# The one-hot product of an expert choice goes to GpSimd, with two one-hot tiles in place of one

## The chip, the cores and the metric

One core of one Trainium2 chip runs the whole program. The time is the device time of one execution in microseconds (us). Engines are called by the profile's names: PE (TensorE; PEld is its weight load), DVE (VectorE), ACT (ScalarE), POOL (GpSimd), SP (SyncE, which here only issues transfers).

## What is computed

Three transformer layers run one after the other on 256 tokens of width 1024, all in f32. The first two layers end in a mixture of 16384 tiny experts, and the change lies there:

```python
q  = (h @ wq).reshape(B, S, PEER_HEADS, 2, half)          # 8 heads, two halves
s1 = einsum('bshd,hnd->bshn', q[..., 0, :], keys[:, 0])   # 128 scores a half
v1, i1 = top_k(s1, 16);  v2, i2 = top_k(s2, 16)
cand = v1[..., :, None] + v2[..., None, :]                # sums of pairs
sc, j = top_k(cand, 16)
e1 = take_along_axis(i1, j // 16); e2 = take_along_axis(i2, j % 16)
experts = e1 * 128 + e2;  gates = softmax(sc)
act = gelu(einsum('td,ted->te', ht, u[experts]))
out = einsum('te,ted->td', gates * act, v[experts])
```

## The kernel before

The kernel is written engine by engine, each engine's instructions in an order fixed by the program, with semaphores between the engines. Nothing is scheduled by a planner.

**The expert layer.** It gathers nothing. It computes `gelu` of h times every row of the table u: 128 blocks of 128 experts, block `j` into column `j` of the array `av`. After that it multiplies `av` by a sparse matrix of gates and multiplies the result by the table v, again in 128 blocks. The profile calls nearly everything in SBUF `mem`, since the tiles are slices of one tensor.

**A u-block.** A table piece of 128x1024 comes by a transfer into a ring. ACT (`hi`) rounds it to `r_sh`, DVE (`lo`) forms the rest `r_sl`. PE's `block_T` multiplies by both: 16 matmuls with `r_sh`, then, after a wait for "lo", 8 with `r_sl`. `r_sh` and `r_sl` have two buffers each, so ACT begins `hi(n)` when PE is done with block n-2. After each block ACT takes its result through `gelu`.

**The choice of experts.** Which experts a token wants is found during these same blocks, on DVE. `choices` is a Python generator: for each of two tiles of 128 tokens it takes 16 top-16 selections of 128 scores (`side`), forms the 50 candidate sums of each head (`cand`) with the numbers of their experts (`ecand`), takes each head's top 16 of 50, and then turns 16 places into 16 expert numbers. For this last step, of each head h: a one-hot tile of 16 x 50 is made by comparing places with `iota` (EQ), multiplied by `ecand` (MUL), and summed over the 50 (`tensor_reduce` into `EF`). All are 128x800 in the trace, and all three used one tile, `hot`.

**What sets the order on DVE.** `peer_ve` walks over `j` = 0 to 127. At each `j`, called a slot below, it issues `lo` of the next block and then as many steps of `choices` as this rule asks for. Each step gives its cost by `yield`; `COST` is their sum, so that the steps end just before `j` = 75:

```python
for j in range(128):
    lo(ve, (U + V)[j + 1])
    while spent * (C_FROM - 3) < COST * (j + 1):     # C_FROM = 78
        did = next(pick, None)
        ...
        spent += did
```

**After the choice.** "e12" (expert numbers split in two) and "gates" (softmax) are awaited by PE's transposes ahead of blocks 76 and 77 ("eTp"); ACT copies these to `eT` at `j` = 77 and 78. Only then does POOL have work in this layer: `peer_po` makes a part of the one-hot tiles `oneA` for the gate matrix. Until then it only helps with the norm ahead of the layer. `J_EARLY` and `J_LATE` say from which block on ACT's `gelu` would write over the tiles of the choice, and what it waits for there.

Of the kernel before, what the change touches and what calls it, by code (L numbers as in the profile page):

```python
# [19 lines left out]
NP = len(PAIRS)  # L20
# [206 lines left out]
MUL, ADD, SUB, MAX, MIN, EQ = ALU.mult, ALU.add, ALU.subtract, ALU.max, ALU.min, ALU.is_equal  # L227
# [58 lines left out]
def build(nc, io, ctx):  # L286
# [28 lines left out]
    def C(name, rows=128):  # L315
        lo, hi = CST[name]
        return cst[0:rows, lo:hi]

    def P(name, i=None):
        lo, hi = COL[name]  # L320
        return col[:, lo:hi] if i is None else col[:, lo + i:lo + i + 1]
# [163 lines left out]
    def norm_po(po, k, gain, shift=None):  # L485
        po.wait_ge("rr", k)
        for c in (3, 7):
            h = hT[:, c, :]
            po.wait_ge(*po.tensor_tensor(h, xT[:, c, :], rr_, MUL).then_inc("scaledP"))
            if shift is None:  # L490
                po.tensor_scalar(h, h, gain(c), MUL).then_inc("hP", k, c)
            else:
                po.tensor_scalar(h, h, gain(c), MUL, shift(c), ADD).then_inc("hP", k, c)
        for c in (3, 7):
            po.wait_ge("hhi", k, c)
            po.tensor_tensor(hlov[:, c, :], hT[:, c, :], hhiv[:, c, :].bitcast(F32), SUB).then_inc("hloP", k, c)
# [32 lines left out]
    o = 0  # L529

    def take(n):
        nonlocal o
        o += n
        return arena[:, o - n:o]
# [354 lines left out]

    av = mem[:, 0:32768].rearrange("p (j t) -> p j t", j=128)  # L890
    A0 = 32768 - A
    o = A0 - (4096 + 6 * 256 + 8 * (3 * 32 + 2 * (NP + 2)) + 700 + 16 * NP) - 4096
    keysb = take(2048)
    keys = keysb.rearrange("p (h n) -> p h n", h=16)
    qTb = [chunks(take(1024), 4) for _ in range(2)]
# [2 lines left out]
    SC, EF, GT, E1, E2 = (take(256) for _ in range(5))  # L898
    EI = take(256).bitcast(U32)
    s2 = [take(128) for _ in range(2)]  # L900
    cand, ecand = (take(8 * (NP + 2)).rearrange("p (h c) -> p h c", h=8) for _ in range(2))
    cand2 = take(NP + 2)[:, 0:NP]
    hot = take(16 * NP)
    v16 = take(256).rearrange("p (h k) -> p h k", h=8)
    i16 = take(256).bitcast(U32).rearrange("p (h k) -> p h k", h=8)
    f16 = take(256).rearrange("p (h k) -> p h k", h=8)
    p16 = take(128).bitcast(U32)
    p16f = take(128)
    st = take(32)
    assert o <= A0, o  # L910
    o = A0
# [8 lines left out]
    iota = C("iota")  # L920
# [8 lines left out]
    def peer(layer):  # L929
        k = 1 + 2 * layer  # L930
# [9 lines left out]
        def raw_tile(src):  # L940
            tiles.append([src, ("raw_free", layer, len(tiles) - 4) if len(tiles) >= 4 else was[0]])
            return len(tiles) - 1
# [9 lines left out]
        for j in range(128):  # L952
            if j < 127:
                V.append(table("v", j + 1))
            if layer == 0 and 4 <= j < 124 and (j - 4) % 2 == 0 and (j - 4) % 10 < 8:
                pc, q = (j - 4) // 10, (j - 4) % 10 // 2
                at, w = flat(WEIGHTS["ada"])[pc]
                i = raw_tile(io["ada"][at:at + 128 * w].rearrange("(p f) -> p f", p=128)[:, 1024 * q:1024 * q + 1024])
# [30 lines left out]
        def peer_po(po):  # L989
            norm_po(po, k, lambda c: P(f"f{layer}", c))  # L990
            po.wait_ge("x_out", layer)
            for g in range(64):
                s = 4 * (g % 2)
                po.wait_ge("eT", layer, g // 32)
                if g >= 2:
                    po.wait_ge("prod", layer, g - 2)
                for i in range(2):
                    n = 4 * g + i
                    d = po.tensor_scalar(oneA[:, s + i, :], iota, eT[0][:, n:n + 1], EQ, eT[2][:, n:n + 1], MUL)
                d.then_inc("hotP", layer, g)  # L1000
# [92 lines left out]
        def side(ve, t, h, i):  # L1093

            s, k0 = scores[:, t, 2 * h + i, :], 16 * i
            va, vb = v16[:, h, k0:k0 + 8], v16[:, h, k0 + 8:k0 + 16]
            ia, ib = i16[:, h, k0:k0 + 8], i16[:, h, k0 + 8:k0 + 16]
            ve.wait_ge("scores", layer, h // 2, t)
            ve.wait_ge(*ve.max(va, s).then_inc("dveC"))
            d = ve.match_replace(s2[i], va, s, -3e38).then_inc("dveC")  # L1100
            ve.max_index(ia, va, s)
            ve.wait_ge(*d)
            ve.wait_ge(*ve.max(vb, s2[i]).then_inc("dveC"))
            return ve.max_index(ib, vb, s2[i]).then_inc("dveC")

        def choices(ve):

            g, s = GT.rearrange("p (h k) -> p h k", h=16), SC.rearrange("p (h k) -> p h k", h=16)
            for t in range(2):
                for h in range(8):  # L1110
                    for i in range(2):
                        d = side(ve, t, h, i)
                        yield 15
                ve.wait_ge(*d)
                ve.wait_ge(*ve.tensor_copy(f16, i16).then_inc("dveC"))
                ve.wait_ge(*ve.tensor_scalar(f16[:, :, 0:16], f16[:, :, 0:16], 128.0, MUL).then_inc("dveC"))
                yield 6
                for dst, src in ((cand, v16), (ecand, f16)):
                    off = 0
                    for i0, i1, n in ((0, 1, 16), (1, 2, 8), (2, 3, 5), (3, 4, 4), (4, 5, 3), (5, 8, 2), (8, 16, 1)):  # L1120
                        m = i1 - i0
                        dv = dst[:, :, off:off + m * n].rearrange("p h (i j) -> p h i j", i=m)
                        x = src[:, :, i0:i1].rearrange("p h (i o) -> p h i o", o=1).broadcast_to([128, 8, m, n])
                        z = src[:, :, 16:16 + n].rearrange("p h (o j) -> p h o j", o=1).broadcast_to([128, 8, m, n])
                        d = ve.tensor_tensor(dv, x, z, ADD)
                        off += m * n
                    d = d.then_inc("dveC")
                    yield 14
                ve.wait_ge(*d)
                for h in range(8):  # L1130
                    c, sc16, p = cand[:, h, 0:NP], SC[:, 128 * t + 16 * h:128 * t + 16 * h + 16], p16[:, 16 * h:16 * h + 16]
                    ve.wait_ge(*ve.max(sc16[:, 0:8], c).then_inc("dveC"))
                    d = ve.match_replace(cand2, sc16[:, 0:8], c, -3e38).then_inc("dveC")
                    ve.max_index(p[:, 0:8], sc16[:, 0:8], c)
                    ve.wait_ge(*d)
                    ve.wait_ge(*ve.max(sc16[:, 8:16], cand2).then_inc("dveC"))
                    d = ve.max_index(p[:, 8:16], sc16[:, 8:16], cand2).then_inc("dveC")
                    yield 13
                ve.wait_ge(*d)
                d = ve.tensor_copy(p16f, p16).then_inc("dveC")  # L1140
                if t:
                    ve.tensor_tensor(g, s, s[:, :, 0:1].broadcast_to([128, 16, 16]), SUB).then_inc("gmax", layer)
                hv = hot.rearrange("p (k c) -> p k c", k=16)
                for h in range(8):
                    ve.wait_ge(*d)
                    i = ve.tensor_tensor(hv, p16f[:, 16 * h:16 * h + 16].rearrange("p (k o) -> p k o", o=1).broadcast_to([128, 16, NP]),
                                         iota[:, 0:NP].rearrange("p (o c) -> p o c", o=1).broadcast_to([128, 16, NP]), EQ).then_inc("dveC")
                    yield 10
                    ve.wait_ge(*i)
                    i = ve.tensor_tensor(hv, hv, ecand[:, h, 0:NP].rearrange("p (o c) -> p o c", o=1).broadcast_to([128, 16, NP]),  # L1150
                                         MUL).then_inc("dveC")
                    yield 10
                    ve.wait_ge(*i)
                    d = ve.tensor_reduce(EF[:, 128 * t + 16 * h:128 * t + 16 * h + 16], hv, ADD).then_inc("dveC")
                    yield 10
            ve.wait_ge(*d)
            ve.wait_ge(*ve.tensor_copy(EI, EF).then_inc("dveC"))
            ve.tensor_scalar(E2.bitcast(U32), EI, 127, ALU.bitwise_and)
            ve.wait_ge(*ve.tensor_scalar(E1.bitcast(U32), EI, 7, ALU.logical_shift_right).then_inc("dveC"))
            ve.tensor_copy(E2, E2.bitcast(U32))  # L1160
            ve.tensor_copy(E1, E1.bitcast(U32)).then_inc("e12", layer)
            yield 15
            ve.wait_ge("gexp", layer)
            ve.wait_ge(*ve.tensor_reduce(st[:, 0:16], g, ADD).then_inc("dveC"))
            ve.wait_ge(*ve.reciprocal(st[:, 16:32], st[:, 0:16]).then_inc("dveC"))
            ve.tensor_tensor(g, g, st[:, 16:32].rearrange("p (h o) -> p h o", o=1).broadcast_to([128, 16, 16]), MUL).then_inc("gates", layer)
            yield 10

        COST = 2 * (16 * 15 + 6 + 28 + 8 * 13 + 8 * 30) + 25

        def peer_ve(ve):
            norm_ve(ve, k, WQ[0][0], lambda c: P(f"f{layer}", c))
# [23 lines left out]
            for j in range(128):  # L1196
                lo(ve, (U + V)[j + 1])
                while spent * (C_FROM - 3) < COST * (j + 1):
                    did = next(pick, None)
# [1102 lines left out]
```

## Time and profile before

| | |
|---|---|
| median of 3 runs | 2711.04 us (2706.79 to 2711.13) |
| the profiled execution | 2704.2 us, of which its span is 2702.4 us |
| PE busy | 2496.0 us, 92% of the span |
| DVE busy | 1720.0 us, 64% |
| ACT busy | 1297.0 us, 48% |
| POOL busy | 466.0 us, 17% |
| u-blocks 2 to 75 or so, first expert layer | about 290 to 520 us of the span |
| the same, second expert layer | about 1374 to 1604 us |

A share is a mean over stages with different limits. What the change is worth has to be read inside the two stretches in the last lines of the table. Matmuls overlap in the records (0.28 us each, started every 0.12 us), so a busy PE says that it had work, and its pace is seen in the distance between starts.

### The profile page before, as it was taken

What the parts mean: (1) busy time and instruction counts of PE and PEld (TensorE: products, weight loads), DVE (VectorE), ACT (ScalarE), POOL (GpSimd) and SP (SyncE); (2) the same over time, 40 slices, a digit from 0 to 9 for tenths busy, and PEclk for the clock granted to TensorE, in tenths of its full rate; (3) what the DMA queues carried; (4) which work ended last, traced back from release to release, by engine and by line L of the source; (5) the groups of instructions that cost most, each with busy time, mean ns of one, the idle gap of its engine ahead of it and who ended that gap; (6) DMA issues with size and microseconds to landing.
All of it is one profiled execution on the core that took longest, in us unless ns stands there. A gap on an engine that the chain in (4) does not pass through costs nothing.

```text
span 2702.4 us, 47390 instructions
## 1 busy us (share of the span) xinstructions
PE 2496.0 (92%) x19556; PEld 2407.8 (89%) x19556; DVE 1720.0 (64%) x3162; ACT 1297.0 (48%) x2447; POOL 466.0 (17%) x390
## 2 busy tenths in 40 slices
PE   7277999999999999888899999999999988997899
PEld 6267999999999999865799999999999977787899
DVE  3864699877777767534469987775555543534654
ACT  4124544576544444444444456654444443453543
POOL 4900000188500000000000018850000000001000
PEclk9668999999999999999899999999999988999999
DMA  6103355544477777530235554446556553223352
GB/s 239 50 32 125 102 182 185 164 133 129 138 265 250 252 240 251 225 125 32 94 125 183 185 172 131 128 141 196 185 182 185 182 212 134 85 94 122 128 187 79
DMA packets 93220, 422.17 MB, mean 156 GB/s; under 512 B 10296, under 2 KB 12880, under 8 KB 85072
## 3 DMA queue, kind: packets, MB, share of 16 engines
q1 hardware_dynamic: 93008, 419.16, 46.8%
q8 instruction: 156, 2.56, 0.4%
q14 instruction: 56, 0.46, 0.0%
HBM read 415.96 MB, written 3.16 MB: 155 GB/s over the span
## 4 chain that ended last, share of the span: by engine, by line
PE 88%; DVE 6%; ACT 4%; issue 1%; POOL 0%; DMA 0%; SPq 0%; DVEq 0%; POOLq 0%; ACTq 0%
PE PS L170 88%; ACT mem L181 2%; DVE mem L192 2%; ACT r_sh L181 1%; DVE mem L184 1%; DVE r_sl L184 1%; DVE hT L192 1%; PE PS L173 0%; DVE mem L204 0%; ACT L180 0%; DVE xT L184 0%; DVE mem L198 0%; ACT r_hhi L181 0%; POOL hT L184 0%; DVE hT L188 0%
## 5 line engine op out<-in xcount | busy, mean ns | idle before, releaser
L184 DVE TENSOR_TENSOR r_sl<-mem,r_sh 128x1024 fp32r<-128x1024 f32 (+3 forms) x742 | 891.8, 1203 | 756.0 <-ACT r_sh L181 753.1
L181 ACT ACTIVATE r_sh<-mem 128x1024 fp32r<-128x1024 f32 (+3 forms) x742 | 765.1, 1033 | 510.7 <-PE PS L170 469.4
L170 PE MATMUL PS<-r_hhi,r_sh 128*128 128x256 f32 x3280 | 840.3, 292 | 101.1 <-ACT r_sh L181 66.4
L170 PE MATMUL PS<-r_hlo,r_sh 128*128 128x256 f32 (+1 forms) x3152 | 790.7, 287 | 17.6 <-DVE r_hlo L184 15.8
L170 PEld LDWEIGHTS PS<-r_hhi,r_sh 128*128 128x128 f32 x3280 | 644.2, 196 | 110.2 <-issue 57.2
L170 PEld LDWEIGHTS PS<-r_hlo,r_sh 128*128 128x128 f32 (+1 forms) x3152 | 616.5, 196 | 20.2 <-DVE r_hlo L184 17.6
L170 PE MATMUL PS<-r_ch,r_sh 128*128 128x256 f32 x2048 | 504.1, 283 | 0.0
L170 PE MATMUL PS<-r_cl,r_sh 128*128 128x256 f32 x2048 | 503.2, 283 | 0.7 <-DVE r_cl L184 0.7
L170 PE MATMUL PS<-r_hhi,r_sl 128*128 128x256 f32 x3280 | 469.9, 286 | 2.0 <-DVE r_sl L184 2.0
L181 ACT ACTIVATE mem<-PS 128x256 f32<-128x256 f32 (+22 forms) x629 | 215.2, 351 | 512.1 <-PE PS L170 485.9
L189 POOL TENSOR_SCALAR xT<-cst,mem 128x128 f32<-128x128 f32 x256 | 327.5, 1291 | 621.9 <-ACT mem L181 558.1
L170 PEld LDWEIGHTS PS<-r_hhi,r_sl 128*128 128x128 f32 x3280 | 431.8, 195 | 2.8 <-DVE r_sl L184 2.5
L170 PEld LDWEIGHTS PS<-r_cl,r_sh 128*128 128x128 f32 x2048 | 393.1, 192 | 1.1 <-DVE r_cl L184 1.1
L170 PEld LDWEIGHTS PS<-r_ch,r_sh 128*128 128x128 f32 x2048 | 393.0, 192 | 0.0
L170 PE MATMUL PS<-r_ch,r_sl 128*128 128x256 f32 x2048 | 289.7, 283 | 0.0
L170 PEld LDWEIGHTS PS<-r_ch,r_sl 128*128 128x128 f32 x2048 | 265.2, 192 | 0.0
L170 PE MATMUL PS<-mem 64*128 64x128 f32 (+8 forms) x824 | 134.5, 319 | 3.2 <-DVE mem L204 1.1
L184 POOL TENSOR_TENSOR hT<-xT,small 128x256 f32<-128x256 f32 x12 | 9.9, 822 | 736.1 <-ACT small L181 736.1
L170 PE MATMUL PS<-xT 128*128 128x128 f32 x1024 | 130.8, 276 | 4.0 <-DVE xT L184 4.0
L170 PEld LDWEIGHTS PS<-mem 64*128 64x128 f32 (+4 forms) x824 | 100.9, 172 | 33.6 <-issue 17.8
L170 PEld LDWEIGHTS PS<-xT 128*128 128x128 f32 x1024 | 123.4, 193 | 4.3 <-issue 4.3
L181 ACT ACTIVATE mem<-mem 128x128 f32<-128x128 f32 (+9 forms) x117 | 62.5, 544 | 134.6 <-DVE mem L198 75.7
(126 smaller groups left out, 2238.2 us busy)
## 6 DMA issues: line engine op xcount, KB each, us to landing
mem<-in_u SPq DMA_DIRECT2D x256, 512.0 KB, 3.6
mem<-in_v SPq DMA_DIRECT2D x256, 512.0 KB, 4.3
mem<-in_w SPq DMA_DIRECT2D x16, 2048.0 KB, 8.2
mem<-in_ada SPq DMA_DIRECT2D x48, 512.0 KB, 4.1
mem<-in_in SPq DMA_DIRECT2D x9, 2048.0 KB, 8.4
mem<-in_wq SPq DMA_DIRECT2D x8, 2048.0 KB, 8.5
mem<-in_od_in SPq DMA_DIRECT2D x6, 2048.0 KB, 9.2
mem<-in_ev_in SPq DMA_DIRECT2D x5, 2048.0 KB, 10.6
```

The source lines that it names most:

```text
L170: return self.did(self.e and self.e.matmul(out, lhsT, rhs, start=start, stop=stop, skip_group_check=skip))
L181: return self.did(self.e and self.e.activation(out, in_, func, **kw))
L184: return self.did(self.e and self.e.tensor_tensor(out, a, b, op))
L189: return self.did(self.e and self.e.tensor_scalar(out, a, s1, s2, op0, op1))
L192: return self.did(self.e and self.e.scalar_tensor_tensor(out=out, in0=a, scalar=s, in1=b, op0=op0, op1=op1))
```

## The change

DVE still makes the one-hot tile of a head (EQ) and still sums it (`tensor_reduce`). The product with `ecand` is now a POOL instruction, 8 a tile, 16 a layer, 32 in all, written ahead of POOL's other work of the layer. There are two one-hot tiles, used in turn. On DVE the sum of head h-1 now stands behind the EQ of head h. EQ announces "asked", POOL's product "found", the sum "chosen"; EQ of head h waits for "chosen" of head h-2, which is two sums back in the tile and the DVE instruction just ahead of it. `COST` is smaller by the steps that left, so all steps of the choice are spread over the same 75 slots at 1101/75 = 14.7 units a slot, where it was 1261/75 = 16.8.

The second tile takes 800 more columns, so all tiles of the choice begin 800 columns lower; with that `J_EARLY` goes from 77 to 74 and `J_LATE` from 93 to 90.

```diff
-    o = A0 - (4096 + 6 * 256 + 8 * (3 * 32 + 2 * (NP + 2)) + 700 + 16 * NP) - 4096
+    o = A0 - (4096 + 6 * 256 + 8 * (3 * 32 + 2 * (NP + 2)) + 700 + 32 * NP) - 4096
...
-    hot = take(16 * NP)
+    hot = [take(16 * NP).rearrange("p (k c) -> p k c", k=16) for _ in range(2)]
...
             po.wait_ge("x_out", layer)
+
+            for t in range(2):
+                for h in range(8):
+                    po.wait_ge("asked", layer, t, h)
+                    po.tensor_tensor(hot[h % 2], hot[h % 2], ecand[:, h, 0:NP].rearrange("p (o c) -> p o c", o=1).broadcast_to([128, 16, NP]),
+                                     MUL).then_inc("found", layer, t, h)
...
-                d = ve.tensor_copy(p16f, p16).then_inc("dveC")
+                ve.tensor_copy(p16f, p16).then_inc("places", layer, t)
...
-                hv = hot.rearrange("p (k c) -> p k c", k=16)
-                for h in range(8):
-                    ve.wait_ge(*d)
-                    i = ve.tensor_tensor(hv, p16f[...], iota[...], EQ).then_inc("dveC")
-                    yield 10
-                    ve.wait_ge(*i)
-                    i = ve.tensor_tensor(hv, hv, ecand[...], MUL).then_inc("dveC")
-                    yield 10
-                    ve.wait_ge(*i)
-                    d = ve.tensor_reduce(EF[:, 128 * t + 16 * h:128 * t + 16 * h + 16], hv, ADD).then_inc("dveC")
-                    yield 10
-            ve.wait_ge(*d)
+                for h in range(9):
+                    if h < 8:
+                        if t or h >= 2:
+                            ve.wait_ge("chosen", layer, (8 * t + h - 2) // 8, (h - 2) % 8)
+                        ve.wait_ge("places", layer, t)
+                        ve.tensor_tensor(hot[h % 2], p16f[...], iota[...], EQ).then_inc("asked", layer, t, h)
+                        yield 10
+                    if h:
+                        ve.wait_ge("found", layer, t, h - 1)
+                        d = ve.tensor_reduce(EF[:, 128 * t + 16 * h - 16:128 * t + 16 * h], hot[(h - 1) % 2], ADD).then_inc("chosen", layer, t, h - 1)
+                        yield 10
+            ve.wait_ge("chosen", layer, 1, 7)
...
-        COST = 2 * (16 * 15 + 6 + 28 + 8 * 13 + 8 * 30) + 25
+        COST = 2 * (16 * 15 + 6 + 28 + 8 * 13 + 8 * 20) + 25
```

How the instructions then stand on DVE, at the start of the second tile's one-hot steps in the first expert layer. `r_sl` is `lo` of a block and opens a slot; `mem<-mem,cst 128x800` is EQ, `mem<-mem 128x800` the product, `TENSOR_REDUCE` the sum. Before:

```order
L195 CAST mem<-mem 128x128
L184 TENSOR_TENSOR mem<-mem 128x256
L184 TENSOR_TENSOR mem<-mem,cst 128x800
L184 TENSOR_TENSOR mem<-mem 128x800
L184 TENSOR_TENSOR r_sl_53<-mem,r_sh_51 128x1024
L198 TENSOR_REDUCE mem<-mem 128x16
L184 TENSOR_TENSOR r_sl_54<-mem,r_sh_52 128x1024
L184 TENSOR_TENSOR mem<-mem,cst 128x800
L184 TENSOR_TENSOR mem<-mem 128x800
```

And with the change, the same place and the cycle of four slots that follows:

```order
L184 TENSOR_TENSOR mem<-mem,cst 128x800
L184 TENSOR_TENSOR r_sl_54<-mem,r_sh_52 128x1024
L184 TENSOR_TENSOR mem<-mem,cst 128x800
L198 TENSOR_REDUCE mem<-mem 128x16
L184 TENSOR_TENSOR r_sl_53<-mem,r_sh_51 128x1024
L184 TENSOR_TENSOR mem<-mem,cst 128x800
L184 TENSOR_TENSOR r_sl_54<-mem,r_sh_52 128x1024
L198 TENSOR_REDUCE mem<-mem 128x16
L184 TENSOR_TENSOR mem<-mem,cst 128x800
L184 TENSOR_TENSOR r_sl_53<-mem,r_sh_51 128x1024
L198 TENSOR_REDUCE mem<-mem 128x16
L184 TENSOR_TENSOR r_sl_54<-mem,r_sh_52 128x1024
```

The products are gone from between EQ and sum, and a head's sum comes two steps and at least one `lo` after its EQ. A slot holds one or two steps, in the pattern [EQ, sum], [EQ], [sum, EQ], [sum].

On POOL, in each of the two expert layers, between the norm and the one-hot tiles of the gate matrix:

```order
 L188 TENSOR_SCALAR hT<-hT,col 128x256
 L184 TENSOR_TENSOR r_hlo<-hT,r_hhi 128x256 x2
+L184 TENSOR_TENSOR mem<-mem 128x800 x16
 L189 TENSOR_SCALAR xT<-cst,mem 128x128 x128
```

Sixteen products came in where POOL had nothing; the instructions around them stand as they did.

## Rows read from the trace of the kernel before

**Rows 1.** Busy time in the two stretches of u-blocks with the choice.
```profile
core 0: us, PE busy (x) PEld busy (x) DVE busy (x) ACT busy (x) POOL busy (x), PEclk, DMA share, GB/s
290.00:510.00 220.00, 219.87 (x1834) 219.66 (x1834) 195.05 (x540) 106.26 (x158) 0.00 (x0) 1.00 0.55 173
1374.00:1594.00 220.00, 219.87 (x1834) 219.66 (x1833) 195.06 (x540) 106.29 (x158) 0.00 (x0) 1.00 0.56 173
475.00:505.00 30.00, 30.00 (x252) 30.00 (x252) 29.03 (x29) 15.53 (x23) 0.00 (x0) 1.00 0.57 180
```

**Rows 2.** All waits from 290 to 505 us: us in total, times, longest.
```profile
ACT mem L181 <- PE PS L170: 113.3, 74, 2.5
DVE r_sl L184 <- ACT r_sh L181: 20.3, 33, 6.5
```

**Rows 3.** PE in order of time: low halves (`r_sl`) of two successive blocks.
```profile
start us, us, engine line op out<-in xcount [idle before <-releaser]
442.66 1.12 PE L170 MATMUL PS<-r_hhi,r_sl 128*128 128x256 f32 x8
...
445.54 1.12 PE L170 MATMUL PS<-r_hhi,r_sl 128*128 128x256 f32 x8
```

**Rows 4.** ACT in order of time: one gelu and the `hi` behind it.
```profile
440.94 0.38 ACT L181 ACTIVATE mem<-PS 128x256 f32<-128x256 f32 x1 [1.55 <-PE PS L170]
441.22 1.05 ACT L181 ACTIVATE r_sh<-mem 128x1024 fp32r<-128x1024 f32 x1
```

**Rows 5.** DVE in order of time: a `lo` with slack, then a stretch of one-hot steps.
```profile
442.30 1.23 DVE L184 TENSOR_TENSOR r_sl<-mem,r_sh 128x1024 fp32r<-128x1024 f32 x1 [0.20 <-ACT r_sh L181]
...
479.94 1.22 DVE L184 TENSOR_TENSOR r_sl<-mem,r_sh 128x1024 fp32r<-128x1024 f32 x1
481.07 0.98 DVE L198 TENSOR_REDUCE mem<-mem 128x16 f32<-128x800 f32 x1
482.08 0.99 DVE L184 TENSOR_TENSOR mem<-mem,cst 128x800 f32<-128x800 f32 x1
482.99 1.22 DVE L184 TENSOR_TENSOR r_sl<-mem,r_sh 128x1024 fp32r<-128x1024 f32 x1
484.13 0.98 DVE L184 TENSOR_TENSOR mem<-mem 128x800 f32<-128x800 f32 x1
```

**Rows 6.** POOL in order of time, in the convolution of the first layer.
```profile
54.61 1.90 POOL L184 TENSOR_TENSOR mem<-mem,col 128x512 f32<-128x512 f32 x1
56.59 1.29 POOL L184 TENSOR_TENSOR mem<-mem 128x512 f32<-128x512 f32 x1
57.97 1.90 POOL L184 TENSOR_TENSOR mem<-mem,col 128x512 f32<-128x512 f32 x1
...
61.32 1.04 POOL L184 TENSOR_TENSOR mem<-mem,col 128x512 f32<-128x512 f32 x1
```

**Rows 7.** DVE in order of time, the same stretch.
```profile
54.18 1.43 DVE L184 TENSOR_TENSOR r_sl<-mem,r_sh 128x1024 fp32r<-128x1024 f32 x1 [1.93 <-ACT r_sh L181]
57.06 1.91 DVE L184 TENSOR_TENSOR r_sl<-mem,r_sh 128x1024 fp32r<-128x1024 f32 x1 [1.45 <-ACT r_sh L181]
```

**Rows 8.** POOL in order of time, third layer: a start behind DVE, a 256-column operation.
```profile
2441.02 0.74 POOL L184 TENSOR_TENSOR hT<-mem 128x256 f32<-128x256 f32 x1 [240.97 <-DVE mem L184]
2442.28 0.73 POOL L184 TENSOR_TENSOR r_hlo<-hT,r_hhi 128x256 fp32r<-128x256 f32 x1 [0.53 <-ACT r_hhi L181]
```

**Rows 9.** DVE in order of time: the operation that released the first of these.
```profile
2440.45 0.43 DVE L184 TENSOR_TENSOR mem<-PS,mem 128x256 f32<-128x256 f32 x1 [0.69 <-PE PS L170]
```

**Rows 10.** DVE and PE in order of time: "gates" written, and the transposes of block 76.
```profile
517.54 0.42 DVE L184 TENSOR_TENSOR mem<-mem 128x256 f32<-128x256 f32 x1
...
518.86 0.49 PE L173 MATMUL PS<-cst,mem 128*128 128x128 f32 x3
...
530.29 2.71 PE L170 MATMUL PS<-xT 128*128 128x128 f32 x16 [1.99 <-DVE xT L184]
```

**Rows 11.** PE in order of time, third layer: one of seven such waits in a row.
```profile
2446.96 0.36 PE L170 MATMUL PS<-r_qa,r_sh 128*128 128x256 f32 x1 [1.05 <-ACT r_sh L181]
```

**Rows 12.** Busy time and granted clock around a short and a long PE wait.
```profile
2446.00:2450.00 4.00, 3.04 (x24) 2.88 (x24) 2.16 (x4) 1.35 (x4) 1.47 (x2) 1.00 0.02 4
528.00:534.00 6.00, 4.01 (x25) 3.84 (x24) 5.69 (x10) 4.04 (x14) 2.47 (x3) 0.79 0.45 122
```

More of the change, by code:

```diff
@@ L1139, in choices @@
                 ve.wait_ge(*d)
-                d = ve.tensor_copy(p16f, p16).then_inc("dveC")
+                ve.tensor_copy(p16f, p16).then_inc("places", layer, t)
                 if t:
                     ve.tensor_tensor(g, s, s[:, :, 0:1].broadcast_to([128, 16, 16]), SUB).then_inc("gmax", layer)
-                hv = hot.rearrange("p (k c) -> p k c", k=16)
-                for h in range(8):
-                    ve.wait_ge(*d)
-                    i = ve.tensor_tensor(hv, p16f[:, 16 * h:16 * h + 16].rearrange("p (k o) -> p k o", o=1).broadcast_to([128, 16, NP]),
-                                         iota[:, 0:NP].rearrange("p (o c) -> p o c", o=1).broadcast_to([128, 16, NP]), EQ).then_inc("dveC")
-                    yield 10
-                    ve.wait_ge(*i)
-                    i = ve.tensor_tensor(hv, hv, ecand[:, h, 0:NP].rearrange("p (o c) -> p o c", o=1).broadcast_to([128, 16, NP]),
-                                         MUL).then_inc("dveC")
-                    yield 10
-                    ve.wait_ge(*i)
-                    d = ve.tensor_reduce(EF[:, 128 * t + 16 * h:128 * t + 16 * h + 16], hv, ADD).then_inc("dveC")
-                    yield 10
-            ve.wait_ge(*d)
+                for h in range(9):
[3 more added lines that the diff above has]
+                        ve.wait_ge("places", layer, t)
+                        ve.tensor_tensor(hot[h % 2], p16f[:, 16 * h:16 * h + 16].rearrange("p (k o) -> p k o", o=1).broadcast_to([128, 16, NP]),
+                                         iota[:, 0:NP].rearrange("p (o c) -> p o c", o=1).broadcast_to([128, 16, NP]), EQ).then_inc("asked", layer, t, h)
+                        yield 10
[4 more added lines that the diff above has]
+            ve.wait_ge("chosen", layer, 1, 7)
             ve.wait_ge(*ve.tensor_copy(EI, EF).then_inc("dveC"))
```

## The prediction

> **What bounds the kernel now.** I read the busy time of the two stretches of u-blocks first. PE is busy for 219.87 of 220 us in both, at the full clock; DVE for 195, POOL for nothing [rows 1]. The list of waits of 290 to 505 us has ACT waiting for PE and DVE for ACT, and no row at all in which PE waits [rows 2]. PE's low halves come 445.54 - 442.66 = 2.88 us apart [rows 3], which is 24 matmuls of 0.12 us. So a slot lasts 2.88 us, PE sets it, and the 31.6 us that the 32 products cost DVE (0.98 us each) are under PE's work. To take them away can give nothing here. What the change can do is make DVE late, so the next thing to read is how late DVE may be.
>
> A block that ends at about 440.74 (442.66 less 16 matmuls) lets ACT do its gelu and then `hi`, at 441.22 for 1.05 us [rows 4]. `lo` follows at 442.30 and is through at 443.53 [rows 5]. PE wants it for the low half at 445.54 [rows 3]. DVE's lead is 2.0 us, and it cannot be more, since `hi` waits for PE. It is the reserve of all that follows.
>
> **DVE without its product.** From start to start DVE spends 1.13 us on a `lo`, 1.01 on a sum ahead of an EQ that waits for it, 0.91 on an EQ ahead of something that doesn't wait for it, 1.14 on another `lo` [rows 5]. The new order repeats in four slots with three heads: [lo, EQ, sum], [lo, EQ], [lo, sum, EQ], [lo, sum]. That is 4 x 1.14 + 3 x 0.91 + 2 x 0.91 + 1.01 = 10.1 us, against 4 x 2.88 = 11.5 us. Alone it fits, with 1.4 us to spare in a cycle (before, 29.03 of 30 us were busy at the one-hot steps [rows 1]). The added wait of a sum for "found" would be hidden too: two steps and a `lo`, some 3 us, lie between a head's EQ and its sum. Queued behind that wait is `lo`, for which PE waits.
>
> **What the product takes on POOL.** No row shows 128x800. A two-tensor operation of 256 columns takes 0.73 us [rows 8] and of 512 columns 1.29 us, while it was ahead of DVE's `lo` [rows 6]: 2.19 ns a column, so 1.29 + 288 x 2.19 ns = 1.92 us. Below lies the form with an operand that is one value per row, 1.04 us for 512 [rows 6]; with the same fixed 0.17 us that gives 0.17 + 800 x 1.70 ns = 1.53 us. Above lies the 0.73 us scaled whole, 800/256 x 0.73 = 2.28 us, as if nothing of it were fixed. I take 1.92: both operands of the new product vary along the columns, as in the 1.29 us row. The GPSIMD Engine Reference of the Trainium skill (section 3.1) gives 2.6 cycles an element for two inputs; at its 1.2 GHz that is an estimate of 1.73 us for 800, by which the sum below would be about 5 us and not 11. The trace's 2.19 ns a column is the same slope; the difference is the fixed part.
>
> **What it takes from DVE.** The rows of the convolution show the two engines excluding each other. `lo` began at 57.06, took 1.91 us in place of 1.23 and ended at 58.97: it really ran from 57.74, which is 0.14 us before POOL's 56.59 + 1.29 = 57.88 [rows 6, 7]. POOL's next operation took 1.90 us in place of 1.04: it ran from 58.83, again 0.14 us before the end of `lo`. The one at 54.61 did the same behind the `lo` that ended at 55.61. So each waits for the other's whole operation, less 0.14 us. `lo` and EQ read two SBUF tensors, like the operations of these rows. The sum reads one; no row has one beside POOL. I take it as free of this. If it isn't, that is the dear rival below. The SBUF page of the Trainium skill (Who interferes with whom) says that a DVE instruction with at most one SBUF input outside the 2-port modes doesn't contend, and a reduction never; no run so far shows it.
>
> POOL starts 0.14 us after DVE's end (2440.45 + 0.43 to 2441.02 [rows 8, 9]). Three places in a cycle then cost DVE a wait, counted from the start of an EQ:
> - [EQ, sum], then `lo`: the product runs from 0.98 + 0.14 = 1.12 and lets go at 1.12 + 1.92 - 0.14 = 2.90. `lo` could start at 1.82. Wait 1.08.
> - [EQ], then `lo`: `lo` is on at 0.91, ahead of POOL. The product runs from 0.91 + 1.23 - 0.14 = 2.00 and lets go at 3.78. The sum starts at 2.05, and the EQ behind it could at 3.06. Wait 0.72.
> - [sum, EQ], `lo`, [sum], `lo`: the same, but the last `lo` could start at 2.96. Wait 0.82.
>
> Together 2.6 us. A cycle is 10.1 + 2.6 = 12.7 us against 11.5: DVE falls back 1.2 us every three heads.
>
> **The walk through the slots.** I carried this on slot by slot: DVE starts `lo` when it and `hi` are ready, PE starts a low half when `lo` is through, and the lead never passes 2.0 us. First tile: the first `lo` behind a lone EQ finds DVE idle and POOL already in and waits 1.4 us; the lead falls from 2.0 to 0.6 us within four slots. Then PE waits 0.60, 0.07, 1.15 and 0.26 us, in sum 2.1. Second tile: the copy of the places and the extra subtraction put the first EQ later, the first `lo` waits the whole 1.8 us, the lead is 0.25, and PE waits 0.94, 0.07, 1.15, 0.07 and 1.10 us, in sum 3.3. (Each 1.1 to 1.2 is one cycle's deficit.) A layer loses 5.3 us, the two 10.7 us.
>
> Does the clock add to it? PE waits of 1.05 us in the third layer, seven in a row, 4.1 us apart, leave the granted clock at 1.00, its upper level [rows 11, 12]. After 2.0 us of waiting at 528.3 it was lower, 0.79 on average over 6 us [rows 10, 12]. The waits forecast here stay below 1.2 us, so I add nothing.
>
> **What costs nothing.** "gates" is written by 517.96, 0.9 us ahead of the transposes of block 76 [rows 10]. In the new order these steps stand in the same slots, 73 and 74, and have only to come before a PE that is itself later; in the walk they are 1.3 us ahead. The "gmax" for ACT's exponential moves from slot 59 to 62 and is wanted at 70. The lower `J_EARLY` and `J_LATE` wait for the last scores and for `eT`, both over by then. POOL's next work is wanted only after "eT". PE, ACT and SP keep their order, and no transfer is added.
>
> **The sum.** 2704.2 us of the profiled execution (span 2702.4 and 1.8 around it) + 10.7 = 2714.9. The median shown lies 6.8 us higher, so I say 2711.04 + 10.7, about 2721.5 us. Each 0.1 us of product above 1.7 is worth 32 x 0.1 = 3.2 us; below 1.6 the lead swallows nearly all: 1.53 gives +0.6, 2.28 gives +22.
>
> **Rivals.**
> - **Hidden after all**, 2711 to 2714. The product is near 1.53 us, or the exclusion costs less than in the convolution, because here POOL's operations come singly. For it: POOL would be busy for about half the time at most, and the break-even product is 1.6 us. Against: the four fits to 0.14 us. Chance 0.28.
> - **A longer product**, some 2.3 us, or PE waits long enough to lower the clock: 2711 + 22 = 2733. Sixteen runs of 50 columns are a shape no row has. Against: nothing in the rows charges for the number of runs. Chance 0.11.
> - **The sum is blocked as well.** Then nothing of the product is under DVE work: another 0.7 us a head by the same walk, +34 us in all, 2745. No row speaks to it. Chance 0.08.
> - **Faster.** PE's one long wait here is the 1.99 us at 530.29 for the first one-hot tiles, with the low clock behind it [rows 10, 12]: some 3.3 us a layer. If an earlier end of the choice removed it, 2704.5. But the new `COST` spreads the steps over the same 75 slots, and the transposes at 518.86 didn't wait; it would need "gates" a slot earlier and the transposes moved. Chance 0.03.
>
> **How the numbers follow.** The likeliest case, PE losing 4 to 17 us because DVE waits for POOL, has 0.5, with 2715 to 2728 as its own range. 0.2% of this time, about what a measurement can tell, is 5.4 us, so the low end of that case counts as no change: I put 0.02 of its chance there. Slower is then 0.48 + 0.11 + 0.08 = 0.67, the same 0.30, faster 0.03. For 8 in 10 the range leaves out the blocked sum and the faster case and half of the tail: 2709 to 2734.
>
> **What would show it.** In the new profile: POOL products of about 1.9 us, longer where a `lo` is ahead; `lo` and EQ in the one-hot slots with some 2 us in place of 1.2 and 1.0, the sums still 0.98; some nine PE waits for `r_sl` a layer, in two clusters near 375 to 410 and 485 to 520 us of the span, 5 us in sum; the rest of the span shifted and otherwise the same. The prediction is wrong if `lo` beside a product keeps its 1.23 us, if the product is off 1.9 us by more than 0.2, or if the sums lengthen.

## The result and the profile after

The changed kernel took 2718.5 us in the median of 20 runs, the kernel before 2708.0 us in the same comparison: a ratio of 1.0033 (95% interval 1.0025 to 1.0041), 8.9 us slower (6.8 to 11.1). Two of the 20 runs of the changed kernel were slow, 3129.5 and 3535.2 us at a granted clock of 0.734 and 0.645 where the other 18 had 0.952 to 0.958; the ratio leaves them out, and the 8.9 us is the ratio times 2708.0, not the distance of the medians (10.5). Its profiled execution took 2713.9 us with a span of 2711.9, 9.5 us more than the span before.

The busy time in the two stretches of u-blocks, which answers to [rows 1]:

```profile
core 0: us, PE busy (x) PEld busy (x) DVE busy (x) ACT busy (x) POOL busy (x), PEclk, DMA share, GB/s
290.00:510.00 220.00, 218.95 (x1821) 218.28 (x1820) 190.13 (x522) 104.74 (x157) 33.62 (x15) 1.00 0.56 171
1380.00:1600.00 220.00, 218.82 (x1818) 217.98 (x1818) 191.92 (x525) 105.17 (x157) 35.83 (x16) 1.00 0.58 174
```

PE has 13 to 16 matmuls fewer in the same 220 us (x1821 and x1818, 1834 before), some 0.12 us each. DVE is only 3 to 5 us less busy, though 15 or 16 products of 0.98 us left it: part of its busy time is now waiting, which the profile counts as busy. The clock is at its upper level throughout, so none of this loss is the clock's.

POOL in order of time, three successive products of the first tile:

```profile
389.65 1.76 POOL L184 TENSOR_TENSOR mem<-mem 128x800 f32<-128x800 f32 x1 [2.07 <-DVE mem L184]
393.48 2.68 POOL L184 TENSOR_TENSOR mem<-mem 128x800 f32<-128x800 f32 x1 [2.07 <-DVE mem L184]
397.09 2.67 POOL L184 TENSOR_TENSOR mem<-mem 128x800 f32<-128x800 f32 x1 [0.93 <-DVE mem L184]
```

The product takes 1.76 us when nothing is ahead of it (14 of the 32), and 2.67 when a `lo` is (18 of the 32). DVE beside these, a cycle of four slots, which answers to [rows 5]:

```profile
389.49 0.97 DVE L198 TENSOR_REDUCE mem<-mem 128x16 f32<-128x800 f32 x1
390.38 2.11 DVE L184 TENSOR_TENSOR r_sl<-mem,r_sh 128x1024 fp32r<-128x1024 f32 x1
392.42 0.98 DVE L184 TENSOR_TENSOR mem<-mem,cst 128x800 f32<-128x800 f32 x1
393.32 1.22 DVE L184 TENSOR_TENSOR r_sl<-mem,r_sh 128x1024 fp32r<-128x1024 f32 x1
394.45 0.97 DVE L198 TENSOR_REDUCE mem<-mem 128x16 f32<-128x800 f32 x1
395.46 1.55 DVE L184 TENSOR_TENSOR mem<-mem,cst 128x800 f32<-128x800 f32 x1
396.93 1.21 DVE L184 TENSOR_TENSOR r_sl<-mem,r_sh 128x1024 fp32r<-128x1024 f32 x1
398.07 0.97 DVE L198 TENSOR_REDUCE mem<-mem 128x16 f32<-128x800 f32 x1
398.96 1.88 DVE L184 TENSOR_TENSOR r_sl<-mem,r_sh 128x1024 fp32r<-128x1024 f32 x1
400.77 0.98 DVE L184 TENSOR_TENSOR mem<-mem,cst 128x800 f32<-128x800 f32 x1
401.67 0.97 DVE L198 TENSOR_REDUCE mem<-mem 128x16 f32<-128x800 f32 x1
402.56 2.10 DVE L184 TENSOR_TENSOR r_sl<-mem,r_sh 128x1024 fp32r<-128x1024 f32 x1
```

Read the second column. The `lo` at 390.38 lasts 2.11 us in place of 1.22: the product ran from 389.65 to 391.41. The EQ at 395.46 lasts 1.55 in place of 0.98, under the product that ended at 396.16. The `lo` at 398.96 lasts 1.88. The sums stay at 0.97, also the one at 389.49, with a product beside it for most of its time. And PE's low halves:

```profile
401.28 1.12 PE L170 MATMUL PS<-r_hhi,r_sl 128*128 128x256 f32 x8
404.72 1.22 PE L170 MATMUL PS<-r_hhi,r_sl 128*128 128x256 f32 x8 [0.40 <-DVE r_sl L184]
407.70 1.12 PE L170 MATMUL PS<-r_hhi,r_sl 128*128 128x256 f32 x8
```

The `lo` at 402.56 was through at 404.66, the low half began at 404.72, 3.44 us after the one before and not 2.88. The same reading of all low halves from 310 to 520 us and from 1395 to 1605 us gives the distances that are over 2.88 us. In us, by which they are over:

| | first tile | second tile | sum |
|---|---|---|---|
| forecast, each layer | 0.60, 0.07, 1.15, 0.26 | 0.94, 0.07, 1.15, 0.07, 1.10 | 5.3 |
| first expert layer | 0.07, 0.56, 0.10, 0.06 | 0.42, 0.09, 0.55, 0.09, 0.22, 0.10 | 2.3 |
| second expert layer | 0.07, 0.56, 0.09, 0.06 | 0.41, 0.10, 0.56, 0.09, 0.22, 0.09 | 2.2 |

(One of 0.35 us a layer, at ACT's exponential, is there before and after and left out.) So the choice costs 4.5 us. Of the 9.5 us by which this span grew, 5 us lie elsewhere, and what they are is taken up behind the experiments on the choice.

### The profile page after: what moved, and what is told of

It reads as the page before. It is cut to its first block, busy times and chain, and to the rows that moved or that the text cites. A ratio compares the mean times of both kernels' runs of the same rounds, so it can differ in the third digit from the quotient of the medians.

```text
span 2711.9 us, 47394 instructions
## 1 busy us (share of the span) xinstructions
PE 2500.0 (92%) x19556; PEld 2408.6 (89%) x19556; DVE 1713.0 (63%) x3130; ACT 1296.5 (48%) x2447; POOL 544.3 (20%) x422
## 4 chain that ended last, share of the span: by engine, by line
PE 83%; DVE 10%; ACT 5%; issue 1%; POOL 1%; DMA 0%; SPq 0%; DVEq 0%; POOLq 0%; ACTq 0%
PE PS L170 83%; DVE r_sl L184 3%; DVE mem L184 2%; ACT mem L181 2%; DVE mem L192 2%; ACT r_sh L181 2%; DVE mem L198 1%; DVE hT L192 0%; ACT L180 0%; POOL r_hlo L184 0%; PE PS L173 0%; DVE mem L204 0%; ACT r_hhi L181 0%; DVE xT L184 0%; POOL hT L184 0%
## 5 line engine op out<-in xcount | busy, mean ns | idle before, releaser
L184 DVE TENSOR_TENSOR r_sl<-mem,r_sh 128x1024 fp32r<-128x1024 f32 (+3 forms) x742 | 911.4, 1229 | 771.8 <-ACT r_sh L181 769.0
L184 POOL TENSOR_TENSOR mem<-mem 128x800 f32<-128x800 f32 (+1 forms) x62 | 115.3, 1860 | 463.1 <-DVE mem L184 460.8
L184 POOL TENSOR_TENSOR hT<-xT,small 128x256 f32<-128x256 f32 x12 | 10.7, 888 | 738.9 <-ACT small L181 738.9
```

What stands on the lines that cost most here:

```text
L184: return self.did(self.e and self.e.tensor_tensor(out, a, b, op))
```

## The experiments

The theory: POOL's product and DVE's two-tensor operations exclude each other, DVE falls behind, and PE waits for `lo`. Rivals: the new order, the second tile or the addresses cost; handing a tile to POOL and back costs by itself; the short waits lower PE's clock. Each ratio below is against runs of the kernel before in the same comparison, and a time in us behind it is the ratio times their median.

### The product back on DVE

```diff
 # as the change, but without the products in peer_po, and
                     if h:
+                        ve.wait_ge("asked", layer, t, h - 1)
+                        ve.tensor_tensor(hot[(h - 1) % 2], hot[(h - 1) % 2], ecand[...], MUL).then_inc("found", layer, t, h - 1)
+                        yield 10
                         ve.wait_ge("found", layer, t, h - 1)
...
-        COST = 2 * (16 * 15 + 6 + 28 + 8 * 13 + 8 * 20) + 25
+        COST = 2 * (16 * 15 + 6 + 28 + 8 * 13 + 8 * 30) + 25
```

> The change without its move: two one-hot tiles, the sum one step behind and the lower addresses stay, but the product is a DVE instruction again (three steps a head, COST 1261 as before). If the loss comes from POOL's products excluding DVE, the time is that of the kernel before, 2708 us within 2, with no PE wait for r_sl in the slots of the choice. If it comes from the new order, the second tile or the addresses, 5 to 9 us of loss stay.

Ratio 0.9999 (0.9990 to 1.0008). The low halves from 305 to 520 us are 2.88 us apart but for the one at ACT's exponential. The order, the second tile and the addresses cost nothing that can be measured, as expected.

### Half of the product

```diff
-                    po.tensor_tensor(hot[h % 2], hot[h % 2], ecand[...].broadcast_to([128, 16, NP]), MUL)
+                    po.tensor_tensor(hot[h % 2][:, 0:8, :], hot[h % 2][:, 0:8, :], ecand[...].broadcast_to([128, 8, NP]), MUL)
```

> The change with a product over 8 of the 16 places of a head, so that half of the numbers are summed without it (the experts chosen are not the reference's; the work elsewhere is the same). By the exclusion the product holds DVE for about 0.95 us in place of 1.76; the slot walk then has no PE wait: the stretch of u-blocks as long as before in both layers. Rival, the handing to and fro between DVE and POOL costs by itself: about the loss of the change stays.

Ratio 1.0001 (0.9992 to 1.0010). This kernel leaves out half of each product. The handing to and fro, with its 32 waits each way, is all there, and the loss is gone. No low half of the choice is late. The half product takes 0.97 us with nothing ahead of it, so it lies inside DVE's slack; the walk puts the break-even at some 1.6 us, and no run lies between 0.97 and 1.76 us to show where it is.

### A longer product

```diff
-                                     MUL).then_inc("found", layer, t, h)
+                                     MUL).then_inc("once", layer, t, h)
+                    po.wait_ge("once", layer, t, h)
+                    po.tensor_tensor(hot[h % 2][:, 0:8, :], hot[h % 2][:, 0:8, :], ones[...].broadcast_to([128, 8, NP]),
+                                     MUL).then_inc("found", layer, t, h)
```

> The change with a second POOL operation behind each product, over 8 of 16 places, times one (same results). It adds some 0.97 us of POOL time a head. By the exclusion with break-even passed, each microsecond a head costs 32 us: some 31 us more than the change, 2748 us, and less if the sum of DVE fills in between. Rival, POOL's time is hidden and something else costs: no more than 3 us more than the change.

Ratio 1.0099 (1.0083 to 1.0114), 26.8 us over the kernel before. Its median is 2732.2 us where 2748 were expected. By the low halves of the first layer PE lost 14.5 us there, so 29 in two. PE's waits from 300 to 1000 us, the change first, then this kernel (in total, times, longest; a PE that still has matmuls in its pipeline shows less waiting than the low halves are late):

```profile
PE PS L170 <- DVE r_sl L184: 1.1, 3, 0.4
```

```profile
PE PS L170 <- DVE r_sl L184: 11.9, 10, 1.6
```

From 4.5 us to 29 us by 0.97 us of POOL a head is 25 us, where 31 were expected; between the two POOL operations DVE gets a turn, and 30 of the 32 second operations last 1.6 to 1.8 us in place of 0.97. The measured times have a smaller step, 26.8 against 8.9 and 6.2 us, so 18 to 21 us: the profile of the change holds some 5 us from outside the choice (below). The loss follows POOL's time, with a slope somewhat under the count.

### A product that nobody waits for

```diff
 # as the kernel before, with a tile `spare` of 800 more columns, EQ announcing "asked", and in peer_po
+            for t in range(2):
+                for h in range(8):
+                    po.wait_ge("asked", layer, t, h)
+                    po.wait_ge(*po.tensor_tensor(spare, iota[...].broadcast_to([128, 16, NP]), iota[...], MUL).then_inc("spared"))
```

> The kernel before, all three steps on DVE, and beside it a POOL product of 128x800 of two other tiles for each head, started with DVE's EQ; nobody waits for its result. Exclusion alone can cost here: DVE's own product and every lo and EQ meet it, with 5.1 us a head of which 4.9 are used already. The slot walk with 1.76 us gives some 19 us a layer, 2742 us. If what costs in the change is the handing over of a tile to POOL and back, this costs nothing, 2706 us.

Ratio 1.0115 (1.0099 to 1.0130), 31 us, where 38 were expected (2742 us over 2704). DVE in order of time:

```profile
379.11 0.99 DVE L184 TENSOR_TENSOR mem<-mem 128x800 f32<-128x800 f32 x1
380.01 2.54 DVE L184 TENSOR_TENSOR r_sl<-mem,r_sh 128x1024 fp32r<-128x1024 f32 x1
382.48 0.97 DVE L198 TENSOR_REDUCE mem<-mem 128x16 f32<-128x800 f32 x1
383.49 0.99 DVE L184 TENSOR_TENSOR mem<-mem,cst 128x800 f32<-128x800 f32 x1
384.40 1.22 DVE L184 TENSOR_TENSOR r_sl<-mem,r_sh 128x1024 fp32r<-128x1024 f32 x1
385.53 2.31 DVE L184 TENSOR_TENSOR mem<-mem 128x800 f32<-128x800 f32 x1
```

and POOL in the same time:

```profile
379.22 2.26 POOL L184 TENSOR_TENSOR mem<-cst 128x800 f32<-128x800 f32 x1 [4.16 <-DVE mem L184]
384.62 2.37 POOL L184 TENSOR_TENSOR mem<-cst 128x800 f32<-128x800 f32 x1 [3.14 <-DVE mem L184]
```

No DVE instruction waits for POOL by a semaphore, and none touches the tile that POOL writes. Still DVE's own product lasts 2.31 us in place of 0.98 and `lo` 2.54 in place of 1.22, always the next two-tensor operation after POOL has got in. With no handing over in this kernel, what is left to explain it is the exclusion. The walk behind the 38 us took 1.76 us for this product. Its two inputs are both `iota`, and it is shorter: the one at 379.22 ended at 381.48 and could run from 379.96, 0.14 us before the end of DVE's product, so 1.52 us. By the walk's own count 32 x 0.24 = 7.7 us come off, which leaves 30.

### Wider slots

```diff
-                        yield 10      # after EQ, and after the sum
+                        yield 13
...
-        COST = 2 * (16 * 15 + 6 + 28 + 8 * 13 + 8 * 20) + 25
+        COST = 2 * (16 * 15 + 6 + 28 + 8 * 13 + 8 * 26) + 25
```

> The change with 13 in place of 10 as the cost of its steps, and COST with it (1197): a head's two steps are spread over 1.63 slots in place of 1.36, the selections are packed closer. DVE gets 4.7 us for a head and needs about 4.4 with its waits for POOL. By the exclusion there is no PE wait for r_sl left in the slots of the choice, with lo and EQ still 0.5 to 1.3 us longer beside a product; the two stretches are 2.2 us shorter each than with the change, and some 4.5 us of its loss are gone. What is left of the loss then has another cause. If the loss isn't from DVE's lateness, the time is that of the change.

Ratio 1.0003 (0.9994 to 1.0012). `lo` is still longer beside a product, here in a slot of the second tile (2.10 us for the `lo`, 1.22 without):

```profile
492.23 0.98 DVE L184 TENSOR_TENSOR mem<-mem,cst 128x800 f32<-128x800 f32 x1
493.13 0.97 DVE L198 TENSOR_REDUCE mem<-mem 128x16 f32<-128x800 f32 x1
494.02 2.10 DVE L184 TENSOR_TENSOR r_sl<-mem,r_sh 128x1024 fp32r<-128x1024 f32 x1
```

PE waits once for it in the first layer (0.5 us, at the exponential), no longer in a cluster. The expectation had no such wait at all. By the low halves that place is late by 1.01 and 0.10 us where the kernel before has 0.35, in both layers, so some 1.5 us are left of the 4.5. The ratio alone can't tell that from nothing; the runs at a mean granted clock of 0.958 bear it out (2705.9 us in ten runs, 2704.3 in twelve of the kernel before). The exclusion is the same; with room for it, it costs little. This is also the plain mending of the change, and it only gets back to the kernel before: the work taken from DVE was hidden, as the first part of the prediction says.

### The change again

> The change itself, unaltered, beside the kernel before on this chip. Its profile showed 4.4 us of PE waiting for r_sl in the choice, yet its median was 9 us up. If the exclusion is all of the loss, this repeat gives 4 to 6 us and a granted clock like that of before (0.958); if the short waits also lower the clock, the loss stays 8 to 10 us and the mean clock is 0.954 to 0.955.

Ratio 1.0023 (1.0014 to 1.0033), 6.2 us. The clock was 0.956 to 0.958 in its ten runs, 0.956 to 0.958 in those of before; in the first comparison, the change had runs down to 0.952. The late low halves are the same to 0.03 us (4.5 us). So the same short waits don't bring the lower mean clock with them, and what the change costs beyond them is not fixed: 1.7 us here, 4.4 in the first comparison. In that comparison time goes with the clock: the changed kernel's run at 0.952 took 2721.7 us and its three at 0.958 took 2709.9 to 2713.5. The clocks of the kernel before are not on record there, so how much of the 4.4 us is clock can't be told.

### Where the rest was: the norms ahead of the layers

The profile of the change and that of before differ ahead of the choice too. In each norm, DVE's `lo` of the next weights and POOL's second operation start within 0.1 us of each other, and in the norms of the two expert layers either can be first. Two more profiles of the kernel before:

> The kernel before, unaltered, for a second profile. Which of lo and POOL's operation goes first in the norms is decided by less than 0.1 us. If it is chance, some of its norms now show POOL's r_hlo of 4 us, as in the profile of the change; if the program decides it, the norms look as in its first profile.

> The kernel before, unaltered, for a third profile, with the same question as in e10: with chance, the outcome differs between looks or between the norms of one look.

Their spans were 2708.4 and 2708.6 us, 6 us over the first profile of the same kernel. POOL and `lo` in the norm of the first expert layer, in the first of these profiles:

```profile
239.27 0.92 POOL L188 TENSOR_SCALAR hT<-hT,col 128x256 f32<-128x256 f32 x1
240.16 1.24 POOL L184 TENSOR_TENSOR hT<-xT,small 128x256 f32<-128x256 f32 x1
241.50 0.97 POOL L188 TENSOR_SCALAR hT<-hT,col 128x256 f32<-128x256 f32 x1
243.53 4.76 POOL L184 TENSOR_TENSOR r_hlo<-hT,r_hhi 128x256 fp32r<-128x256 f32 x2 [1.06 <-ACT r_hhi L181]
239.34 1.47 DVE L184 TENSOR_TENSOR r_sl<-mem,r_sh 128x1024 fp32r<-128x1024 f32 x1 [7.00 <-ACT r_sh L181]
```

and in the profile of before that the prediction was made from:

```profile
239.60 2.00 POOL L188 TENSOR_SCALAR hT<-hT,col 128x256 f32<-128x256 f32 x1
241.57 0.83 POOL L184 TENSOR_TENSOR hT<-xT,small 128x256 f32<-128x256 f32 x1
242.51 0.97 POOL L188 TENSOR_SCALAR hT<-hT,col 128x256 f32<-128x256 f32 x1
243.53 0.76 POOL L184 TENSOR_TENSOR r_hlo<-hT,r_hhi 128x256 fp32r<-128x256 f32 x1
239.67 1.23 DVE L184 TENSOR_TENSOR r_sl<-mem,r_sh 128x1024 fp32r<-128x1024 f32 x1 [7.00 <-ACT r_sh L181]
```

One kernel, two outcomes. Where POOL gets its TENSOR_SCALAR in ahead of `lo` (0.92 us, and `lo` 1.47), it later stands behind a chain of DVE's subtractions with its `r_hlo` (4.76 us for two), and PE waits 1.75 us for POOL; where `lo` is first (2.00 us, and `lo` 1.23), that wait is missing. Other waits of the norm get shorter for it: PE's waits for `r_hhi` and `r_hlo` together come to 9.35 us in the first case and 7.96 in the second, so the outcome is worth 1.4 us a norm.

The profile of the change had the first outcome in both norms of the expert layers, as both new profiles of the kernel before had, and the first profile of before in neither. So the change isn't needed for it. Over all ten profiles of kernels with `lo` ahead, those of the experiments above included, six have it in the first of these norms and five in the second, and the half product has one of each. Whether it falls anew at each execution is not shown: the two new profiles of the kernel before, on one chip, agree with each other, and so do the two of the change.

One more place can be read in the same profiles. Ahead of the third layer PE sums squares for a norm with 16 matmuls. Before, their row and the stretch around them (busy time and clock):

```profile
2184.57 3.69 PE L170 MATMUL PS<-hT,cst 128*128 128x256 f32 x16 [0.97 <-ACT hT L181]
2182.00:2189.00 7.00, 4.49 (x18) 3.07 (x18) 0.94 (x6) 3.63 (x10) 0.00 (x0) 1.00 0.36 102
```

and with the change:

```profile
2190.33 6.67 PE L170 MATMUL PS<-hT,cst 128*128 128x256 f32 x16 [0.97 <-ACT hT L181]
2188.00:2197.00 9.00, 7.47 (x18) 5.19 (x18) 0.69 (x5) 2.93 (x9) 0.00 (x0) 0.62 0.53 162
```

In the 2.9 us ahead of them PE had only two small matmuls (0.8 us) in both profiles, yet in one the clock stood at its upper level and in the other it had fallen: 3.0 us. All three profiles of the kernel before have 3.69 us here, the two of the change 6.67 and 6.68. But the next experiment, on the kernel before, has 6.71 and the last one, on the change, 3.69, so it doesn't go with the products, and its cause is open.

With this the 9.5 us between the two spans are roughly laid out: 4.5 in the choice, 2.8 in the two norms, 3.0 here, less 0.8 in other places.

### lo behind the norm

```diff
     def norm_ve(ve, k, n, gain, shift=None):
-        lo(ve, n)
         ve.wait_ge("rr", k)
...
                 ve.tensor_tensor(hlov[:, c, :], hT[:, c, :], hhiv[:, c, :].bitcast(F32), SUB).then_inc("hlo", k, c)
+        lo(ve, n)
```

> The kernel before with one line moved in the six norms: lo of the first block behind the norm's other DVE work and not ahead of it. In the profiles so far lo and POOL's operation start within 0.1 us of each other there and either may go first, worth 1 to 2.4 us a norm to PE. With lo last DVE writes each chunk of h 1.14 us earlier and lo no longer stands in POOL's way: 6 x 1.1 us or more, 2699 us or less. Rival, lo is then late for the low half of the first block, or POOL's own chunk is what PE waits for: no gain or a loss of 1 us a norm.

Ratio 0.9960 (0.9946 to 0.9974) with this edit on the kernel before: 10.8 us faster than it, and the fastest kernel of the study together with the next two. PE's waits for ACT in all norms went from 34.5 us to 23.3, those for DVE's `r_hlo` rose from 15.8 to 18.8, and its wait for POOL's `r_hlo` (1.7) is gone: 9.9 us fewer. These are against the first profile of before, which had the better outcome in both norms of the expert layers, and there too the waits fell, from 7.96 to 6.79 us in the first. So most of the gain is `lo` out of the way of DVE's own chunks, which ACT and PE wait for, and not the collision that no longer happens. In the order of time POOL's operations in the first expert layer's norm are now all near their shortest:

```profile
236.66 0.97 POOL L188 TENSOR_SCALAR hT<-hT,col 128x256 f32<-128x256 f32 x1
237.59 0.84 POOL L184 TENSOR_TENSOR hT<-xT,small 128x256 f32<-128x256 f32 x1
238.53 0.97 POOL L188 TENSOR_SCALAR hT<-hT,col 128x256 f32<-128x256 f32 x1
239.47 0.84 POOL L184 TENSOR_TENSOR r_hlo<-hT,r_hhi 128x256 fp32r<-128x256 f32 x1
```

> The change with wider slots (13 a step) and lo last in the norms. If both act alone as read, the time is that of the norm edit on the kernel before within 2 us: the wider slots give back the change's loss and no more, since PE sets the pace in the choice either way.

Ratio 0.9975 (0.9965 to 0.9984), 6.8 us faster than before. Expected was the same as the edit on the kernel before within 2 us, which is 4 us off.

> The change, with lo last in the norms, slots as in the change. With the collision in the norms gone on both sides, what it loses against the norm edit on the kernel before is the choice's part alone. By the slot count that is 4.4 us: 2700 us where e7 had 2695.5. If 8 us or more are left, the rest of the change's loss isn't from the norms.

Ratio 0.9959 (0.9946 to 0.9973), as good as the edit on the kernel before, where it should have been 4.5 us behind. That is a miss. Part of it can be read. Busy time and clock of the first layer, ahead of any choice, in the profile of the edit on the kernel before:

```profile
0.00:40.00 40.00, 25.04 (x151) 23.12 (x152) 15.13 (x22) 18.74 (x33) 12.32 (x25) 0.87 0.70 277
190.00:235.00 45.00, 33.91 (x214) 31.41 (x212) 17.95 (x27) 22.21 (x35) 0.00 (x0) 0.81 0.26 97
```

and in that of the edit on the change:

```profile
0.00:40.00 40.00, 24.87 (x160) 23.26 (x161) 15.93 (x22) 18.84 (x33) 12.30 (x25) 0.91 0.70 277
190.00:235.00 45.00, 31.46 (x210) 28.88 (x209) 20.12 (x31) 24.20 (x39) 3.13 (x4) 0.88 0.31 117
```

The same instructions ran at a granted clock of 0.91 and 0.88 where the other had 0.87 and 0.81, and the norm of the first expert layer began 4.2 us earlier (231.66 against 235.82 us, POOL's first operation in it). The 16 matmuls ahead of the third layer took 3.0 us less as well. In the choice the late low halves are there as in the change, 0.06 to 0.57 us each. Why the clock differs in a stage with the same instructions is open.

The runs say the same once they are put side by side by their mean granted clock. The first four kernels of this table ran in one comparison on one chip, the last two rows come from another comparison on another chip:

| kernel | mean at a lower clock | mean at a higher clock |
|---|---|---|
| kernel before | 2704.4 us at 0.957 (4 runs) | 2704.5 at 0.958 (13) |
| the change | 2712.2 at 0.957 (4) | 2710.6 at 0.958 (5) |
| norm edit on the kernel before | 2695.5 at 0.958 (3) | 2686.8 at 0.962 (1) |
| norm edit, the change, wider slots | 2700.8 at 0.958 (3) | 2695.8 at 0.961 (3) |
| kernel before, other chip | 2709.2 at 0.956 (5) | 2708.0 at 0.957 (3) |
| norm edit on the change, other chip | 2702.2 at 0.958 (1) | 2696.5 at 0.962 (3) |

At the same clock the kernel before was 2 to 4 us slower on the other chip (at 0.956, where the first chip's two runs took 2707.5, and at 0.957). Taking that off, the norm edit on the change is 3 to 8 us behind the norm edit alone, in place of level with it. So the 4.5 us of the choice are most likely still there and were hidden by a clock that four of its five runs had and only one of the five others; with single runs in two cells that is a reading, not a measurement. The kernel with wider slots is 5 us behind the norm edit alone at 0.958; the late places at the exponential give 1.5 of these, and no run shows the rest.

## Why the prediction came out

Slower was forecast, by 10.7 us, and slower it was, by 8.9 (6.8 to 11.1) and, repeated, by 6.2 (3.8 to 8.9). The steps, one by one:

- **What DVE saves is hidden.** Right: with the exclusion out of the way (half product) or nearly so (wider slots) the time is that of before, not less.
- **Each engine waits for the other's whole operation, less 0.14 us.** Right, and to a few hundredths. With 1.76 in the place of 1.92 the three waits of a cycle come to 0.92, 0.56 and 0.66 us; the rows show `lo` 2.11 - 1.22 = 0.89, EQ 1.55 - 0.98 = 0.57 and `lo` 1.88 - 1.22 = 0.66. The product that nobody waits for showed it with no semaphore between the engines.
- **The sum is not blocked.** Right: 0.97 us beside products, 0.98 before. The SBUF page of the Trainium skill (Who interferes with whom) says that a reduction never contends; the rows agree. The dear rival, +34 us, is out.
- **The product takes 1.92 us.** This term was mis-sized: it takes 1.76. The slope for each column, taken from the rows of 256 and 512 columns, was too steep: half a product, 400 columns, takes 0.97 us, so this shape has 1.98 ns a column and 0.18 us fixed where the sum had 2.19 and 0.17. The estimate worked out from the GPSIMD Engine Reference of the Trainium skill (section 3.1), 1.73 us, is nearer.
- **The walk through the slots.** The pattern was right, nine or ten late low halves a layer in two clusters, each cycle with one large one. The sizes followed the product: each 0.1 us counts 3.2 us, and with 1.76 the same walk gives 5.6 us in place of 10.7; 4.5 were measured. Some 0.4 of the last 1.1 us is the first wait of the second tile: 1.42 us (`lo` of 2.64 us) where I had 1.8, so 1.64 with the shorter product. The first tile's was as counted, 1.28 (`lo` of 2.50 us) where I had 1.4, so 1.24. The rest is not traced.
- **The clock stays up.** Right in the choice (1.00). Over the whole kernel it differs between executions, 0.952 to 0.958 in the change's 18 runs, and their times by 11.8 us, more than the change is worth.
- **The rest of the span is otherwise the same.** Wrong: 5 of the 9.5 us between the two profiles lie outside the choice.

So the sum came near the measured time while its one term was more than twice what the trace shows. As far as the size goes, that is luck: the mechanism and the way were right, and the choice alone would have given 4.5 us. What fills the gap, 1.7 us in one comparison and 4.4 in the other, is what the forecast did not name: the order of two engines in the norms and the granted clock in other stages. Both differ between profiles of the kernel before too, and its 20 runs spread over 8 us. That they were no more than chance in the 20 runs of the change is not shown. The combined kernels (0.9975 and 0.9959, the wrong way round) say that differences of 4 us between programs can't be read from such medians alone.

## What to carry to other kernels

Before work goes from VectorE to GpSimd, list which VectorE operations beside it read two SBUF tensors, and add GpSimd's whole duration to the next of them. If VectorE is ahead of the bound by less than that, the move costs although it takes work away; giving the slots that room took the cost down to some 1.5 us here, and nothing is the best that it could be while PE sets the pace. An operation that isn't wanted yet (`lo` in the norms) belongs behind those that another engine waits for; that took one moved line and gave 0.4%. And where runs of one program differ in their mean granted clock, compare runs of the same clock before a few microseconds are laid at a change's door.

## What was not expected of the hardware

- Single spans of one kernel differed by 6 us (2702.4 and 2708.4). Who came first in two norms makes 2.8 of these; the rest lies in other places and is not traced. The late low halves of the choice, by contrast, repeated to 0.03 us.
- Sixteen matmuls with the same wait ahead of them took 3.69 us in one profile and 6.67 in another, by the clock that they were granted.
- The product of 128x800, with one operand repeated over 16 runs of 50 columns, shows no charge for the runs: 1.76 us, and 0.97 for half of it. With both operands repeated, as in the product that nobody waits for, it took 1.52 us.
